# Delta-rule diagonal blocks: from DMA round trips through DRAM to VectorE transposes inside SBUF

## The chip, the cores and the metric

The kernel runs on one core of one Trainium2 chip. A core has five engines that run their own instruction streams in order and meet only at semaphores: TensorE (PE, matrix products, results in PSUM), VectorE (DVE), ScalarE (ACT), GpSimd (POOL) and SyncE (SP, which here only issues DMAs). The metric is device time in microseconds of one execution. The kernel before takes 2107.66 us (median of 3 runs, 2107.57 to 2107.68).

## The reference, cut to what matters

Two blocks of a network on 256 tokens of width 2048. The first is a hybrid layer: one large input projection, an mLSTM branch, a gated delta-rule branch, and output projections. The second is attention with context. The change touches only the delta-rule branch, 16 heads of width 128. Per head it solves a unit triangular system and then runs a recurrence:

```
kk = einsum('cbhtd,cbhsd->cbhts', kc, kc)
a_mat = where(strict, bc[..., :, None] * kk * decay_mat, 0.0)
lhs = a_mat + eye(CHUNK)
sol = triangular_solve(lhs, rhs, left_side=True, lower=True, unit_diagonal=True)
...
u = wv - einsum('bhtd,bhde->bhte', wk, S)
o = einsum('bhtd,bhde->bhte', qd, S) + einsum('bhts,bhse->bhte', qk_c, u)
S_new = ge[..., None, None] * S + einsum('bhsd,bhse->bhde', ke, u)
```

The kernel takes chunks of 128 tokens instead of 64, which gives the same result, so each head has two 128x128 triangular matrices to invert.

## The kernel before, in words

**Slots.** All weights of the projections (608 loads of 512 KB) stream through once. A part of 2048 x 512 is a *unit*, cut into 8 *slots* of 256 x 512; there are 608 slots (`SLOTS`). Per slot SP loads the tile `raw` (5 buffers), ACT copies it to a rounded `WH` (L1900), DVE writes the rest `WL` = raw - WH (L1904), and PE does 24 matmuls with 256 columns (L1960) or 12 with 512 columns (L1956). ACT and DVE prepare slot s+3 in their turn s (`AHEAD` = 3). Units 0 to 11 are `qkv`: for each group n of four heads (a *quad*) q, k and v. Units 12 to 15 are `dnz`, and more follow.

**Stages.** All other work is written as generators, one per engine; `timetable()` lists after which slots each takes its next step (a step is what stands between two `yield`s). Every engine walks the same list: slot s, then the steps planned for s. An engine that waits in a step holds everything later in its stream, its own part of the next slots too. POOL has no slot work, so for it the list only sets an order.

**The convolution stages** (`conv_*`, one per qkv unit, from the unit's last slot on): ACT copies the unit out of PSUM and scales it (L648), DVE adds three taps for each of four tiles (L683, one tile per step), ACT takes a tanh (L654), DVE writes q, k or v (L692; `vv` for v). For q and k ACT squares (L661), PE sums (L705), ACT takes the root (L666, L669) and POOL scales `qk` (L717).

**The quad stages.** Let e be the last slot of the quad's v unit. The steps lie at e+6 to e+10 and at e+20 to e+28. The next quad's q unit ends at e+8 and its k unit at e+16, so its convolution steps run between them, and e+24 is the next quad's e.

- PE: at e+7 transposes of v (L735, step `tv`), at e+8 and e+9 the score products of two heads each (L744, L745, steps `k0` to `k3`).
- POOL: at e+6 loads the decay rows `E` by DMA (L943), for quads 1 to 3 only after the last step `o1` of the quad before, since `E` is reused for `W1`, `U1` and `R2`.
- DVE: at e+7 subtracts and masks in `E` (L875, L880), ACT takes the exponential (L832); at e+8 and e+9 DVE multiplies scores and decays into `PT` and `NT` (L895, `p0` to `p3`). `NT` holds the negated triangular matrices.
- The eight 128x128 matrices have four 32x32 diagonal blocks each. SP (`quad_sp`, after `p3`) sends the 32 blocks to DRAM (L975, 8 DMAs), and reads them back so that each of the 128 partitions holds one block, four times over (L979, 4 DMAs, tile `NB`). POOL starts from unit columns `XB` (L953) and does 31 steps of forward substitution, a multiply (L960) and an add (L963) each, 62 instructions: each partition works on 8 columns of one inverse. SP sends the columns to DRAM (L985) and back into `XT` (L990), and DVE transposes them into `X` (L903, three instructions), at e+20.
- PE, ACT and DVE then join the blocks: `y5` (L756, at e+21, waits for `X`), `z5` (L768, L770), `y6` (L777), `z6` (L785), and apply the inverse and the recurrence (L792 to L820, the last at e+28). ACT (L859 to L865) and DVE (L933, step `o1`) normalise the output.

Of the kernel before, what the change touches and what calls it, by code (L numbers as in the profile page):

```python
# [96 lines left out]
def timetable():  # L97
# [13 lines left out]
    for n in range(4):  # L111
        steps(("quad", n), end("qkv", 3 * n + 2) + 6, 5)
        steps(("quad", n), end("qkv", 3 * n + 2) + 20, 9)
# [27 lines left out]


LEAD = 8
# [9 lines left out]
def hybrid_program(nc, A, out):  # L153
    with ExitStack() as ctx:
# [19 lines left out]
        def pad(n, k):  # L174
# [81 lines left out]
        Z = overlay(16 * KB,  # L256
                    [("wm0", [128, 2, 512], F32), ("wm1", [128, 2, 512], F32), ("macc", [128, 2, 512], F32)],
# [9 lines left out]
        X, XT, XB, TB, Y6, vt, U2, sq, OB = (R[n] for n in ("X", "XT", "XB", "TB", "Y6", "vt", "U2", "sq", "OB"))  # L267
# [10 lines left out]
        W1, U1, R2 = (E[:, :, 128 * i:128 * i + 128] for i in range(3))  # L278
# [278 lines left out]
        def gates_pool(e):  # L557
# [5 lines left out]
            yield  # L563

# [47 lines left out]
        def condition_dve(e):  # L612
# [111 lines left out]

        def above(B, w, h, c):

            return NT[2 * w * B:2 * w * B + w, h, 256 * c + 2 * w * B + w:256 * c + 2 * w * B + 2 * w]

        def quad_pe(e, bank, n):
            yield  # L730
# [20 lines left out]
            e.wait_ge(*qd_dve.at("x", n))  # L751
            claim(e, bank, 0, qd_act.at("y5", n))
            claim(e, bank, 1, qd_dve.at("y5", n))
            for m in range(8):
                for B in range(2):
                    p = e.matmul(SB[B][64 * B + 32:64 * B + 64, 32 * m:32 * m + 32], above(B, 32, m % 4, m // 4),  # L756
# [19 lines left out]
            for m in range(8):  # L776
                p = e.matmul(SB[0][64:128, 64 * m:64 * m + 64], above(0, 64, m % 4, m // 4), X[0:64, m, 0:64],  # L777
# [11 lines left out]
            e.wait_ge(*qd_dve.at("z6", n))  # L789
            claim(e, bank, 0, qd_dve.at("U", n))  # L790
            for h in range(4):
                m = e.matmul(SB[0][:, 128 * h:128 * h + 128], XT[:, h, :], vt[:, 0, h, :], start=True, stop=True,  # L792
                             skip_group_check=True)
# [11 lines left out]
            for h in range(4):  # L805
                m = e.matmul(SB[2][:, 128 * h:128 * h + 128], XT[:, 4 + h, :], R2[:, h, :], start=True, stop=True,
# [17 lines left out]
        def quad_act(e, n):  # L824
            yield
# [7 lines left out]
            for _ in range(5):  # L833
                yield
# [33 lines left out]
        def quad_dve(e, n):  # L868
            yield
# [15 lines left out]
            for h in range(4):  # L885
# [1325 lines left out]
```

## Time and profile before

| | |
|---|---|
| median of 3 runs | 2107.66 us |
| the profiled execution's own time | 2115.09 us |
| its span | 2113.3 us |
| PE busy | 1953.2 us (92%) |
| DVE busy | 1377.1 us (65%) |
| ACT busy | 944.5 us (45%) |
| POOL busy | 221.8 us (10%) |
| DMA mean | 187 GB/s |

The span is what the profiler sees between the first and the last instruction. The profiled execution was 7.4 us longer than the median of the unprofiled runs. PE is the engine with the most work; of its busy time most is the weight products (L1956, L1960). Its idle time and the stretches in which its clock is halved are where a change off the products can be seen.

### The profile page before, as it was taken

What the parts mean: (1) busy time and instruction counts of PE and PEld (TensorE: products, weight loads), DVE (VectorE), ACT (ScalarE), POOL (GpSimd) and SP (SyncE); (2) the same over time, 40 slices, a digit from 0 to 9 for tenths busy, and PEclk for the clock granted to TensorE, in tenths of its full rate; (3) what the DMA queues carried; (4) which work ended last, traced back from release to release, by engine and by line L of the source; (5) the groups of instructions that cost most, each with busy time, mean ns of one, the idle gap of its engine ahead of it and who ended that gap; (6) DMA issues with size and microseconds to landing.
All of it is one profiled execution on the core that took longest, in us unless ns stands there. A gap on an engine that the chain in (4) does not pass through costs nothing.

```text
span 2113.3 us, 29349 instructions
## 1 busy us (share of the span) xinstructions
PE 1953.2 (92%) x11910; PEld 1717.3 (81%) x11910; DVE 1377.1 (65%) x1919; ACT 944.5 (45%) x1336; POOL 221.8 (10%) x425
## 2 busy tenths in 40 slices
PE   5995978859699999999999999999999999999997
PEld 5995867857588889897788878898998998988875
DVE  4674555745378888787876756766455566656574
ACT  4553634434253333343444436464333345545443
POOL 1004040222201111101010100010000000011000
PEclk9997988979899999999999999999999999999998
DMA  6454443524458887767687875676556533454553
GB/s 212 131 153 117 129 132 95 172 77 151 122 193 280 270 271 256 237 221 243 227 282 253 282 262 173 218 230 198 180 169 200 179 122 128 144 166 130 170 199 120
DMA packets 198743, 395.90 MB, mean 187 GB/s; under 512 B 26136, under 2 KB 26416, under 8 KB 197456
## 3 DMA queue, kind: packets, MB, share of 16 engines
q1 hardware_dynamic: 180320, 325.63, 47.9%
q0 software_dynamic: 17424, 66.72, 10.5%
q8 instruction: 94, 1.54, 0.3%
q10 hardware_dynamic: 864, 1.67, 0.2%
q14 instruction: 41, 0.34, 0.1%
HBM read 388.70 MB, written 5.27 MB: 186 GB/s over the span
## 4 chain that ended last, share of the span: by engine, by line
PE 71%; DVE 9%; issue 8%; POOL 5%; ACT 4%; DMA 2%; SPq 1%; ACTq 0%; DVEq 0%; POOLq 0%
PE GB L1956 43%; PE GB L1960 21%; DVE WL L1904 2%; POOL XB L963 2%; POOL TB L960 2%; ACT WH L1900 2%; DVE macc L1280 1%; PE SB L357 1%; PE SB L1586 1%; PE SB L1298 1%; DVE yth L683 1%; PE SB L1578 1%; DMA wm<-in_w_mod 1%; DMA xin<-in_x 1%; DMA inverse_columns<-XB 0%
## 5 line engine op out<-in xcount | busy, mean ns | idle before, releaser
L1904 DVE TENSOR_TENSOR WL<-raw,WH 128x1024 fp32r<-128x1024 f32 x608 | 741.8, 1240 | 291.2 <-ACT WH L1900 288.7
L1900 ACT ACTIVATE WH<-raw 128x1024 fp32r<-128x1024 f32 x608 | 627.4, 1057 | 444.4 <-PE GB L1956 289.4
L1956 PE MATMUL GB<-WH,uH 128*128 128x512 f32 x896 | 283.8, 398 | 1.7 <-DVE WL L1904 1.7
L1956 PE MATMUL GB<-WH,uL 128*128 128x512 f32 x896 | 278.4, 392 | 0.0
L1956 PE MATMUL GB<-WL,uH 128*128 128x512 f32 x896 | 277.8, 391 | 0.0
L1960 PE MATMUL GB<-uH,WH 128*128 128x256 f32 x1280 | 215.7, 291 | 3.8 <-DVE WL L1904 3.8
L1280 DVE SCALAR_TENSOR_TENSOR macc<-wm,csil,macc 128x512 f32<-128x512 f32 x300 | 209.4, 747 | 5.4 <-DMA wm<-in_w_mod 3.9
L1960 PE MATMUL GB<-uL,WH 128*128 128x256 f32 x1280 | 208.7, 286 | 0.0
L1960 PE MATMUL GB<-uH,WL 128*128 128x256 f32 x1280 | 208.4, 286 | 0.0
L1956 PEld LDWEIGHTS GB<-WL,uH 128*128 128x128 f32 x896 | 169.4, 189 | 36.3
L1956 PEld LDWEIGHTS GB<-WH,uL 128*128 128x128 f32 x896 | 169.3, 189 | 36.2
L1956 PEld LDWEIGHTS GB<-WH,uH 128*128 128x128 f32 x896 | 165.7, 190 | 34.1 <-DVE WL L1904 2.6
L1960 PEld LDWEIGHTS GB<-uH,WH 128*128 128x128 f32 x1280 | 180.4, 195 | 8.5 <-issue 5.8
L1960 PEld LDWEIGHTS GB<-uL,WH 128*128 128x128 f32 x1280 | 179.7, 195 | 0.0
L1960 PEld LDWEIGHTS GB<-uH,WL 128*128 128x128 f32 x1280 | 179.5, 195 | 0.0
L1956 PE MATMUL GB<-WH,hH 128*128 128x512 f32 x512 | 162.9, 399 | 0.0
L1956 PE MATMUL GB<-WH,hL 128*128 128x512 f32 x512 | 158.2, 390 | 0.0
L1956 PE MATMUL GB<-WL,hH 128*128 128x512 f32 x512 | 157.8, 389 | 0.0
L1251 POOL DMA_DIRECT2D wm<-in_w_mod x96 | 69.5, 724 | 595.0 <-DVE macc L1280 583.4
L1956 PEld LDWEIGHTS GB<-WL,hH 128*128 128x128 f32 x512 | 96.1, 188 | 20.6
L1956 PEld LDWEIGHTS GB<-WH,hL 128*128 128x128 f32 x512 | 96.1, 188 | 20.4
L1956 PEld LDWEIGHTS GB<-WH,hH 128*128 128x128 f32 x512 | 94.4, 188 | 20.9 <-issue 3.1
(394 smaller groups left out, 2163.8 us busy)
## 6 DMA issues: line engine op xcount, KB each, us to landing
raw<-in_w_in SPq DMA_DIRECT2D x512, 512.0 KB, 4.5
wm<-in_w_mod POOLq DMA_DIRECT2D x96, 512.0 KB, 5.8
raw<-in_w_out SPq DMA_DIRECT2D x96, 512.0 KB, 5.3
xin<-in_x SPq DMA_DIRECT2D x4, 512.0 KB, 6.7
E<-decay_rows POOLq DMA_DIRECT2D x4, 512.0 KB, 5.0
NB<-diagonal_blocks SPq DMA_DIRECT2D x16, 128.0 KB, 2.6
hres<-in_x POOLq DMA_DIRECT2D x1, 2048.0 KB, 12.1
cin<-in_ctx POOLq DMA_DIRECT2D x1, 2048.0 KB, 8.6
```

The source lines that it names most:

```text
L357: t = e.transpose(SB[b][:, 256 * j + 128 * i:256 * j + 128 * i + 128], src[:, i, 128 * (2 * k + j):128 * (2 * k + j) + 128], ident[:, :])
L683: e.scalar_tensor_tensor(out=y[:, j, sh:], in0=half(banks[j // 2], j % 2)[:, 0:256 - sh], scalar=col(CONV + 48 * (3 - sh) + 16 * kind + 4 ...
L960: e.tensor_tensor(TB[:, 0:J, 0:r], NB[:, k:k + 1, k + 1:32].to_broadcast([128, J, r]), XB[:, 0:J, k:k + 1].to_broadcast([128, J, r]), mul) ...
L963: e.tensor_tensor(XB[:, 0:J, k + 1:32], XB[:, 0:J, k + 1:32], TB[:, 0:J, 0:r], add).then_inc(*qd_pool.inc(f"a{k}", n))
L1251: e.dma_start(wmr[n % 2][:, :, :], weights["w_mod"][:, 2 * i:2 * i + 2, 512 * g:512 * g + 512]).then_inc(wm_in[n % 2], 16)
L1280: w = e.scalar_tensor_tensor(out=a, in0=src, scalar=s, in1=a, op0=mul, op1=add)
L1298: m = e.matmul(SB[0][:, 4 * v + j:4 * v + j + 1], macc[:, v, 128 * j:128 * j + 128], ones[:, 0:1], start=True, stop=True, skip_group_check ...
L1578: m = e.matmul(SB[3][:, 0:128], aT[:, n % 2, 128 * q:128 * q + 128], v, start=q == 0, stop=q == 3, skip_group_check=True)
L1900: e.activation(WH[s % NH][:, :, :], raw[s % NR][:, :, :], ACT.Copy).then_inc(*wh.inc("WH", s))
L1904: e.tensor_tensor(WL[s % NH][:, :, :], raw[s % NR][:, :, :], f32(WH[s % NH][:, :, :]), sub).then_inc(*wl.inc("WL", s))
L1956: m = e.matmul(banks[j][:, :], x[:, c, 128 * j:128 * j + 128], w[:, k, :], start=first, stop=last, skip_group_check=True)
L1960: m = e.matmul(half(banks[j // 2], j % 2), w[:, k, 128 * j:128 * j + 128], x[:, c, :], start=first and j % 2 == 0, stop=last, skip_group_c ...
```

## The change

- SP no longer takes part: `quad_sp`, the two DRAM tensors and all 28 DMAs per quad go.
- ACT copies the diagonal blocks side by side into `NTd` (four instructions of 32x256), DVE spreads them with one 128x1024 transpose into `NB` (the input is read four times over). Partition 32b + 4m + g now holds block b of matrix m.
- After the substitution DVE transposes `XB` into `X` (four instructions of 32x256), and `X` into `XT` (four more). PE's `y5` waits for the first two of the eight.
- The quad's first step moves from e+7 to e+6 (the empty first step goes), and everything up to the scores with it. POOL's substitution stands at e+9, ahead of POOL's scaling of the next quad's q (L717), where it stood at e+20.
- `W1`, `U1`, `R2`, `U2` get a place of their own, so that `E` for the next quad can be loaded right behind the substitution. The modulation's first loads now wait for `o1` of quad 3 on PE, since they reuse that place.

```diff
-        steps(("quad", n), end("qkv", 3 * n + 2) + 6, 5)
+        steps(("quad", n), end("qkv", 3 * n + 2) + 6, 4)
         steps(("quad", n), end("qkv", 3 * n + 2) + 20, 9)
...
         def quad_pe(e, bank, n):
-            yield
             e.wait_ge(*cv_dve.at("dst", 3 * n + 2))
...
-            e.wait_ge(*qd_dve.at("x", n))
+            e.wait_ge(*qd_dve.at("x02", n))
...
         def quad_act(e, n):
-            yield
...
-            for _ in range(5):
-                yield
+            yield
+            yield
+            yield
+            e.wait_ge(*qd_dve.at("p3", n))
+            if n:
+                e.wait_ge(*qd_dve.at("nb", n - 1))
+            for b in range(4):
+                q = slice(32 * b, 32 * b + 32)
+                a = e.activation(NTd[q, :, :].rearrange("p (h c) r -> p h c r", c=2),
+                                 NT[q, :, :].rearrange("p h (c t) -> p h c t", c=2)[:, :, :, q], ACT.Copy)
+            a.then_inc(*qd_act.inc("nd", n))
+            yield
+            yield
...
         def quad_dve(e, n):
-            yield
...
-            yield
-            e.wait_ge(inverses_in, 64 * (n + 1))
-            for b in range(3):
+            e.wait_ge(*qd_act.at("nd", n))
+            if n:
+                e.wait_ge(*qd_pool.at("a30", n - 1))
+            e.transpose(NB[:, :, :].rearrange("p k r -> p r k"),
+                        NTd[:, :, :].rearrange("p m r -> p r m").unsqueeze(3).to_broadcast([128, 32, 8, 4]),
+                        ).then_inc(*qd_dve.inc("nb", n))
+            yield
+            e.wait_ge(*qd_pool.at("a30", n))
+            for b in (0, 2, 1, 3):
                 q = slice(32 * b, 32 * b + 32)
-                v = e.transpose(X[q, :, q], XT[q, :, q])
+                v = e.transpose(X[q, :, q].rearrange("p m (j g) -> p j m g", g=4), XB[q, :, :])
+                if b == 2:
+                    v.then_inc(*qd_dve.inc("x02", n))
             v.then_inc(*qd_dve.inc("x", n))
+            e.wait_ge(*qd_dve.at("x", n))
+            for b in (1, 3, 0, 2):
+                q = slice(32 * b, 32 * b + 32)
+                v = e.transpose(XT[q, :, q], X[q, :, q])
+                if b == 3:
+                    v.then_inc(*qd_dve.inc("xt13", n))
+            v.then_inc(*qd_dve.inc("xt", n))
...
         def quad_pool(e, n):
-            if n == 0:
-                e.wait_ge(rows_out, 32)
-                e.wait_ge(*g_dve.at("colG"))
-            else:
-                e.wait_ge(*qd_dve.at("o1", n - 1))
-            e.dma_start(E[:, :, 0:256], rowGd[4 * n:4 * n + 4, :].partition_broadcast(128)).then_inc(rowG_in, 16)
+            yield
+            yield
             yield
...
-            for _ in range(4):
-                yield
-            if n:
-                e.wait_ge(inverses_out, 64 * n)
+            else:
+                e.wait_ge(*qd_dve.at("x", n - 1))
             e.tensor_copy(XB[:, :, :], unit_cols[:, :, :]).then_inc(*qd_pool.inc("unit", n))
             e.wait_ge(*qd_pool.at("unit", n))
-            e.wait_ge(blocks_in, 64 * (n + 1))
+            e.wait_ge(*qd_dve.at("nb", n))
...
-            yield
-
-        def quad_sp(e, n):
...
+            if n < 3:
+                e.wait_ge(*qd_dve.at("p3", n))
+                decays_pool(e, n + 1)
             yield
...
                     if n == 0:
+                        e.wait_ge(*qd_pe.at("o1", 3))
                         load(0)
```

Three places show the moves. Line numbers of the changed kernel differ by a few. First DVE at the start of quad 0, before (L692 and in the changed kernel L689 write `vv`, L1904 and L1902 write `WL`):

```order
L1904 TENSOR_TENSOR WL<-raw,WH 128x1024
L692 SCALAR_TENSOR_TENSOR vv<-yth 128x1024
L1904 TENSOR_TENSOR WL<-raw,WH 128x1024 x2
L875 SCALAR_TENSOR_TENSOR E<-E,colG,mask 128x128 x4
L880 SCALAR_TENSOR_TENSOR E<-E,colG,mask 128x256 x4
L1904 TENSOR_TENSOR WL<-raw,WH 128x1024
L895 SCALAR_TENSOR_TENSOR PT<-SB,E 128x256
```

and now:

```order
L1902 TENSOR_TENSOR WL<-raw,WH 128x1024
L689 SCALAR_TENSOR_TENSOR vv<-yth 128x1024
L1902 TENSOR_TENSOR WL<-raw,WH 128x1024
L883 SCALAR_TENSOR_TENSOR E<-E,colG,mask 128x128 x4
L888 SCALAR_TENSOR_TENSOR E<-E,colG,mask 128x256 x4
L1902 TENSOR_TENSOR WL<-raw,WH 128x1024
L903 SCALAR_TENSOR_TENSOR PT<-SB,E 128x256
```

The decays stand behind one `WL` instead of two: one slot earlier in the stream. (The scores of all four heads then follow one slot earlier too, and behind the last of them, one `WL` and three taps later, stands the new `NB` transpose.)

Second, DVE at e+20 of quad 0, before:

```order
L683 SCALAR_TENSOR_TENSOR yth<-GB,vcol,yth 128x253
L903 STREAM_TRANSPOSE X<-XT 32x8x32 x3
L1904 TENSOR_TENSOR WL<-raw,WH 128x1024
L692 SCALAR_TENSOR_TENSOR qk<-yth 128x1024
L907 COPY Y<-SB 32x256
L1904 TENSOR_TENSOR WL<-raw,WH 128x1024
L910 COPY XT<-SB 32x8x32
```

and now:

```order
L680 SCALAR_TENSOR_TENSOR yth<-GB,vcol,yth 128x253
L917 STREAM_TRANSPOSE X<-XB 32x8x8x4 x4
L924 STREAM_TRANSPOSE XT<-X 32x8x32 x4
L1902 TENSOR_TENSOR WL<-raw,WH 128x1024
L689 SCALAR_TENSOR_TENSOR qk<-yth 128x1024
L930 COPY Y<-SB 32x256
L1902 TENSOR_TENSOR WL<-raw,WH 128x1024
L933 COPY XT<-SB 32x8x32
```

The step has eight transposes where it had three, and the next `WL`, the write of the next k (L689) and the copy into `Y` for `z5` stand behind all of them.

Third, POOL from the end of quad 0's substitution to the start of quad 1's, before:

```order
L960 TENSOR_TENSOR TB<-NB,XB 128x8
L963 TENSOR_TENSOR XB<-XB,TB 128x8
L717 TENSOR_TENSOR qk<-qk,sq 128x1024
L943 DMA E<-decay_rows 128x4x256
L717 TENSOR_TENSOR qk<-qk,sq 128x1024
L953 COPY XB<-unit_cols 128x256
```

and now:

```order
L980 TENSOR_TENSOR TB<-NB,XB 128x8
L983 TENSOR_TENSOR XB<-XB,TB 128x8
L961 DMA E<-decay_rows 128x4x256
L714 TENSOR_TENSOR qk<-qk,sq 128x1024 x2
L973 COPY XB<-unit_cols 128x256
L980 TENSOR_TENSOR TB<-NB,XB 128x31
```

The load of `E` has moved ahead of both scalings of `qk`, and both scalings, the next q and k of quad 1 (kinds 0 and 1), stand between two substitutions. The scaling of quad 1's q stood ahead of quad 0's substitution, that of quad 2's q ahead of quad 1's.

## Rows read from the trace of the kernel before

**Rows 1.** The page: its first line, and in part 6 the modulation's load.

```profile
span 2113.3 us, 29349 instructions
...
wm<-in_w_mod POOLq DMA_DIRECT2D x96, 512.0 KB, 5.8
```

**Rows 2.** What PE waited for: us in total, times, longest.

```profile
PE SB L756 <- DVE X L903: 92.4, 4, 24.4
...
PE SB L744 <- DVE NT L895: 7.8, 4, 3.4
```

**Rows 3.** Chain that ended last, 240 to 360 us: start, us, what.

```profile
324.76 0.43 DVE X L903
...
325.70 1.06 PE SB L756 x32
326.76 4.91 PE GB L1960 x24
...
335.37 1.72 PE SB L705 x4
...
350.02 2.87 PE GB L1960 x24
```

**Rows 4.** PE's timeline, quad 1: start, length, form, idle before it and releaser.

```profile
251.56 1.09 PE L735 MATMUL SB<-ident,vv 128*128 128x128 f32 x8 [0.36 <-DVE vv L692]
...
262.18 1.13 PE L744 MATMUL SB<-qk 128*128 128x512 f32 x2 [1.21 <-DVE NT L895]
...
264.44 0.59 PE L745 MATMUL SB<-qk 128*128 128x256 f32 x2
```

**Rows 5.** DVE's timeline, quad 1, 250 to 303 us.

```profile
250.29 1.22 DVE L692 SCALAR_TENSOR_TENSOR vv<-yth 128x1024 f32<-128x1024 f32 x1
...
255.55 1.67 DVE L880 SCALAR_TENSOR_TENSOR E<-E,colG,mask 128x256 f32<-128x256 f32 x4
...
267.49 0.74 DVE L895 SCALAR_TENSOR_TENSOR NT<-SB,colNB,E 128x256 f32<-128x256 f32 x2
...
294.54 1.22 DVE L1904 TENSOR_TENSOR WL<-raw,WH 128x1024 fp32r<-128x1024 f32 x1
295.67 1.51 DVE L683 SCALAR_TENSOR_TENSOR yth<-GB,vcol,yth 128x255 f32<-128x255 f32 x3
...
300.86 1.50 DVE L683 SCALAR_TENSOR_TENSOR yth<-GB,vcol,yth 128x255 f32<-128x255 f32 x3
```

**Rows 6.** POOL's timeline, quad 1, 287 to 325 us.

```profile
292.19 1.09 POOL L960 TENSOR_TENSOR TB<-NB,XB 128x31 f32<-128x31 f32 x1
...
294.33 0.24 POOL L960 TENSOR_TENSOR TB<-NB,XB 128x29 f32<-128x29 f32 x1
294.65 1.19 POOL L963 TENSOR_TENSOR XB<-XB,TB 128x29 f32<-128x29 f32 x1
...
317.73 0.22 POOL L963 TENSOR_TENSOR XB<-XB,TB 128x8 f32<-128x8 f32 x1
```

**Rows 7.** Lines L836 and L903: ns min/median/max, first and last start, form.

```profile
L836 ACT ACTIVATE Y<-SB x4: 375/375/378, 211.9 to 558.0; 32x256 f32<-32x256 f32 x4
...
L903 DVE STREAM_TRANSPOSE X<-XT x12: 432/434/436, 207.0 to 556.4; 32x256 f32<-32x256 f32 x12
```

**Rows 8.** PE's timeline at four other waits.

```profile
82.16 3.45 PE L705 MATMUL SB<-sq,ones 128*128 128x512 f32 x4 [2.56 <-ACT sq L661]
...
380.42 1.12 PE L744 MATMUL SB<-qk 128*128 128x512 f32 x2 [2.66 <-DVE NT L895]
...
499.44 2.08 PE L744 MATMUL SB<-qk 128*128 128x512 f32 x2 [3.43 <-DVE NT L895]
...
556.85 1.06 PE L756 MATMUL SB<-X,NT 32*32 32x32 f32 x32 [19.17 <-DVE X L903]
```

**Rows 9.** DVE's timeline, quad 3, 485 to 545 us.

```profile
505.50 0.73 DVE L895 SCALAR_TENSOR_TENSOR NT<-SB,colNB,E 128x256 f32<-128x256 f32 x2
...
527.40 5.12 DVE L1904 TENSOR_TENSOR WL<-raw,WH 128x1024 fp32r<-128x1024 f32 x4
```

More of the change, by code:

```diff
@@ L140 @@
 PLAN = timetable()
-LEAD = 8
 def take_turns(stages, s):
@@ L256, in hybrid_program @@
         Z = overlay(16 * KB,
+                    [("W1", [128, 4, 128], F32), ("U1", [128, 4, 128], F32), ("R2", [128, 4, 128], F32),
+                     ("U2", [128, 4, 128], F32), ("NTd", [128, 8, 32], F32)],
                     [("wm0", [128, 2, 512], F32), ("wm1", [128, 2, 512], F32), ("macc", [128, 2, 512], F32)],
@@ L266, in hybrid_program @@
         qk, vv, yth, E, PT, NT, NB = (R[n] for n in ("qk", "vv", "yth", "E", "PT", "NT", "NB"))
-        X, XT, XB, TB, Y6, vt, U2, sq, OB = (R[n] for n in ("X", "XT", "XB", "TB", "Y6", "vt", "U2", "sq", "OB"))
+        X, XT, XB, TB, Y6, vt, sq, OB = (R[n] for n in ("X", "XT", "XB", "TB", "Y6", "vt", "sq", "OB"))
+        W1, U1, R2, U2, NTd = (Z[n][:, :, :] for n in ("W1", "U1", "R2", "U2", "NTd"))
         s_junk, wsm, wsH, wsL, rw, xin = (R[n] for n in ("s_junk", "wsm", "wsH", "wsL", "rw", "xin"))
@@ L277, in hybrid_program @@
         fg, gmat = Z["fg"], Z["gmat"]
-        W1, U1, R2 = (E[:, :, 128 * i:128 * i + 128] for i in range(3))
         zth = yth[:, 0, :, :].rearrange("p (a b) t -> p a (b t)", a=2)
@@ L563, in gates_pool @@
             yield
+            yield
+            e.wait_ge(rows_out, 32)
+            e.wait_ge(*g_dve.at("colG"))
+            decays_pool(e, 0)
+            yield
         def newton_dve(e, says, o, v, w, root):
@@ L789, in quad_pe @@
             e.wait_ge(*qd_dve.at("z6", n))
+            e.wait_ge(*qd_act.at("z6", n))
             claim(e, bank, 0, qd_dve.at("U", n))
             for h in range(4):
-                m = e.matmul(SB[0][:, 128 * h:128 * h + 128], XT[:, h, :], vt[:, 0, h, :], start=True, stop=True,
+                m = e.matmul(SB[0][:, 128 * h:128 * h + 128], XT[:, 2 * h, :], vt[:, 0, h, :], start=True, stop=True,
                              skip_group_check=True)
@@ L805, in quad_pe @@
             for h in range(4):
-                m = e.matmul(SB[2][:, 128 * h:128 * h + 128], XT[:, 4 + h, :], R2[:, h, :], start=True, stop=True,
+                m = e.matmul(SB[2][:, 128 * h:128 * h + 128], XT[:, 2 * h + 1, :], R2[:, h, :], start=True, stop=True,
                              skip_group_check=True)
@@ L2027, in _ @@
                                 x_rows[:, i, 1024 * j:1024 * j + 1024]).then_inc(x_in[2 * i + j], 16)
-            stages = {("quad", n): quad_sp(e, n) for n in range(4)}
             for s in range(NS):
@@ L2036, in _ @@
                             weights[unit.w][:, r:r + 2, unit.col:unit.col + 512]).then_inc(raw_in[s % NR], 16)
-                if s >= LEAD:
-                    take_turns(stages, s - LEAD)
             for j in range(2):
```

46 lines of the change are left out of this document (11 added, 35 removed).

## The prediction

> **What bounds the kernel now.** I read the waits of PE first. Over the whole run one wait stands out: PE waits for `X` before `y5` four times, once per quad, 92.4 us together, 24.4 at most [rows 2]. The one of quad 3 is 19.17 us [rows 8], so the other three are 24.4 each. All other waits in the quads are small; the next is that for `p0` before `k2`, 7.8 us in four.
>
> The chain that ended last shows what lies behind it. In quad 1 it runs through POOL's substitution, SP, the DMA back into `XT`, DVE's `X` at 324.76 and PE's `y5` at 325.70 [rows 3]. The substitution takes from 292.19 to 317.95 [rows 6], and the two DMA legs behind it until the first transpose, 324.3. PE was at `y5` at 301.3 (325.70 - 24.4). DVE was there at 302.36 [rows 5] and also stood, since the wait is in its stream, so no new `WL` came either. The price is more than the idle time: the 24 products behind `y5` take 4.91 us where they take 2.87 later [rows 3], which is the half clock (1.2 instead of 2.4 GHz) for about 2 us of loss.
>
> **The change, worked out on quad 1.** I use the clock times of the profile and keep the transposes `tv` at 251.56 [rows 4] fixed. They wait for `vv`, which DVE ends at 251.5 [rows 5], and nothing ahead of `vv` changes. But `tv` now stands one slot (2.9 us) earlier in PE's stream: PE had 0.36 us to wait, now it has 3.2. This is a new wait, 4 times.
>
> 1. PE behind `tv`: 0.9, a slot 2.9, `k0`, `k1` 2.4 (in rows 4 `k2`, `k3` take from 262.18 to 264.7, where the next product starts), a slot 2.9: it is at `k2` at 260.7.
> 2. DVE: `vv` 251.5, one `WL` 1.1, decays 2.8 (in [rows 5] the last four end at 257.2 behind two `WL` and a wait for the load of `E`, which is now long done), so 255.4. ACT's exponential and `WH`, DVE's `WL` and `p0` follow: in the profile `p0` ends 4.9 behind the decays (257.2, and `k2` starts on it at 262.18), so now at 260.3, and `p1` 1.3 later. `k2` no longer waits (1.21 before, rows 4); `k3` ends at 263.1 against 264.7, one slot earlier in the stream.
> 3. `WL` 1.1, then `p2` and `p3` 2.6: 265.4, against 268.2 [rows 5].
> 4. ACT copies the blocks: 4 x 0.375 by an ACT copy of 32x256 [rows 7] = 1.5, done at 266.9. DVE does a `WL` and three taps meanwhile and is free at 268.0, so this copy is hidden; without that cover it would cost its 1.5.
> 5. The `NB` transpose. No row has one of 128x1024. Between 1.1 us (a `WL` of 1024 elements, rows 5) and 1.74 (four times 32x256 at 0.434, rows 7), and up to 3 if its strides cost. I take 1.5, near the transposes' own rate: 269.5.
> 6. The substitution. Its 62 instructions took 25.8 us [rows 6], but not evenly: the same kind of add takes 0.24 at 294.33 and 1.19 at 294.65, exactly where DVE's `WL` starts at 294.54. It happens at each `WL`, four times here, 0.9 us each, and not beside the taps (at 295.67) [rows 5]. So 25.8 - 3.6 = 22.2 us alone, of which most ran while DVE stood. Now DVE works all the time: one `WL` per slot of 2.9 us takes 0.9 away, so it becomes (22.2 + 0.9 for the write of q) / (1 - 0.9/2.9) = 33.5. End: 303.0 instead of 317.95.
> 7. DVE's own arrival at the step: 302.36 before, now 1.4 later, by the transpose and by PE's small delays ahead of the sums of squares: 303.8. So DVE, not POOL, comes last by a little. Two transposes, 0.9: `y5` at 304.7. PE is there at 263.1 + 13 slots x 2.87 + 1.7 for the sums (L705, rows 3) = 302.1. It waits 2.6 to 3.
> 8. Behind it, DVE has six more transposes (2.6), a `WL`, the write of k (1.2) and the copy for `z5` (0.4, taken as a transpose of that size, rows 7): 5.5 after `y5` starts. PE has 1.06 + 2.9 = 4.0 of work: a second new wait of 1.5. Then `z5` 0.6 and a slot, so the next L705 is at 313.7, where it was at 335.37 [rows 3]. The gain of quad 1 is 21.7 us.
>
> From there to the next `tv` nothing changes: `vv` of the next quad hangs on ACT's and DVE's normalisation behind `o1`, which starts from PE's `o1`. So the quads add up.
>
> - Quad 0: the same waits but for `k2`: 21.6.
> - Quad 2: `k2` waited 2.66 [rows 8], 1.45 more than in quad 1, and this goes too: 23.1.
> - Quad 3 lies beside `dnz` units, where DVE has few other stages, so DVE runs ahead of PE: it came to the `X` step at 532.5 [rows 9], PE at 537.7. The scores ended at 506.2 [rows 9]; they move up by most of the 3.43 us that `k2` waited and of the half clock behind it (the score matmuls took twice their time, 2.08 against 1.13 for a pair, rows 8 and 4, so 2.5 more for all), so `p3` ends near 501.2, POOL starts at 504.4, works 23 us beside DVE and 8 alone and ends at 535.7, with `X` at 536.6 and PE there at 533.5. The 19.17 become 3.1, and with the 3.43, the 2.5 and -2.9 for `tv` the gain is 19.1.
>
> Sum: 21.6 + 21.7 + 23.1 + 19.1 = 85.5 us.
>
> What works against it is PE's clock. Four long idle times become eight short ones of about 3 us. After 2.56 us of idle time PE came back at half clock (L705 took 3.45, and 1.72 in rows 3), after 2.66 it did not, after 3.43 it did [rows 8]. So at 3 us I count 6 in 10. A drop costs 1.5 to 2.5 us, say 2: for `tv` 4 x 0.6 x 2 = 4.8; for `y5` of quads 0 to 2 most of it is hidden in the wait for `z5`, 0.9 in all. This takes 5.7: gain 80.
>
> The rest costs nothing here. SP's 28 DMAs per quad go; they stood behind 10 loads of `raw`, and in the profile DVE was late only by its own wait. The load of `E` now comes behind a substitution and is needed only slots later. ACT's wait for `p3` holds a `WH` that is needed two slots later. The first loads of the modulation wait for `o1` of quad 3, three slots (8.6 us) ahead of DVE's use, and take 5.8 us [rows 1]: covered by about 2; uncovered they would cost up to 6, once.
>
> The profiled execution took 2115.09 us, 1.8 over its span of 2113.3 [rows 1] and 7.4 over the median; this would become about 2035. Taken from the median: 2107.7 - 80 = **2027 to 2028 us**; I say 2027.5.
>
> Step 5 is where a page speaks against the change. The rows show only transposes that write runs of 32 elements at 0.434 us for 256 columns [rows 7]; the new one reads and writes with a stride of 32 elements. The Trainium skill, Vector Engine (DVE) Microarchitecture Reference, section 5.2, says that a port which hops at every element costs more time per column, 1.7 to 2.5 ns instead of 1.05. By that the transpose would take an estimated 2.6 us, and the sum would fall by about 1 us per quad, 4 in all; no row here shows it.
>
> **The rivals.**
>
> *The wait only shrinks (0.17).* The substitution is slower beside a busy DVE than in step 6, since four instructions slowed by one `WL` each are all I have. If decays, writes of q and k, and the `NB` transposes cost it as well, or the 0.9 is 1.2, the 33.5 become 38 to 40, `y5` waits 8 us instead of 3 and the clock falls each time. The gain is 80 - 4 x 5 - 4 x 1 = 56: 2052. For it: step 7 has under 1 us of slack between POOL and DVE. Against it: the four excess times are alike.
>
> *All of it goes (0.12).* DVE catches up, `tv` finds the clock high, `y5` waits for nothing. Then the 92.4 us and 4 x 2.3 us of half clock come back, 101, less the `tv` waits of 4 x 2.9: about 90, 2018. Against it: `vv` really ends at 251.5.
>
> *Only the DMA legs go (0.03).* If the substitution began no earlier (317.95 to 324.3 is all that is saved), 6.4 x 4 = 26: 2082. Against it: the order has the substitution ahead of POOL's scaling, and `NB` hangs on nothing but `p3`.
>
> *Slower (0.03).* POOL comes to a near stop beside DVE: if every DVE instruction, the taps too, holds one of POOL's as long as a `WL` does, nearly each of the 62 takes 1.2 us, 76 us in all, and `y5` comes at 269.5 + 76 = 346 against 325.7: 20 us later per quad, 2187. It is slower from the point where the substitution takes 55 us. Against it: 0.24 at 294.33, with taps of DVE before and after. By the Trainium skill, GPSIMD Engine Reference, Key points, only DVE instructions with two SBUF inputs or in a two-port mode contend with POOL; the taps read one input from PSUM, and the trace agrees.
>
> **How the numbers follow.** The forecast has 0.65, the rivals 0.17, 0.12, 0.03 and 0.03. The range from 2015 to 2047 holds the forecast with its bounds (transpose up to 3 us: +6; all clock drops or none: +6, -6; POOL's 0.9 up to 1.1: +8) and the second rival, and half of the way to the first. What a measurement of this kernel can tell from no change is about 0.2%, 4 us; only the last rival is slower by more, and none lies within: faster 0.96, same 0.01, slower 0.03.
>
> **What would show it.** Right: PE's wait for `X` 2 to 5 us per quad; a wait of about 3 us before the transposes of `vv`; the substitution 31 to 36 us long, starting 3 to 5 us behind `p3`, with a slow instruction at each `WL`; a wait before `z5`. Wrong: the `NB` transpose over 3 us; PE's wait for `X` over 8; substitution under 28; new waits of PE for `WL`, which would mean that eight transposes more than fill DVE; a wait of DVE for the modulation's first load.

## The result, and the profile after

| | before | after |
|---|---|---|
| median of 4 runs each | 2107.67 us | 2039.47 us (2038.58 to 2042.45) |
| ratio, 95% interval | | 0.9679 (0.9662 to 0.9695) |
| the profiled execution, its span | 2115.09, 2113.3 us | 2042.45, 2040.6 us |
| mean granted clock | 0.969 | 0.987 |

The change takes 68.2 us off the median. The forecast was 80 us, 2027.5; the measured time lies in the range, 12 us above the forecast. Between the two profiled executions the gain is 72.64 us, since that of before lay 7.4 us over its median and that of after 3.0.

What PE waited for after (us in total, times, longest), to set beside [rows 2]:

```profile
PE SB L733 <- DVE vv L689: 12.9, 4, 3.5
PE SB L754 <- DVE X L917: 9.6, 4, 5.0
PE SB L766 <- ACT Y L845: 8.6, 3, 2.9
```

The 92.4 us for `X` are 9.6. Two waits are new or much larger: 12.9 before the transposes of v (1.9 before) and 8.6 before `z5` (none before). In what follows `tv` stands for the transposes of v, `k2` for the scores of the third head, and "the sums" for PE's sums of squares of the next quad's k (L705, now L702). PE's timeline in quad 1, where [rows 3, 4] had `tv` at 251.56, `y5` at 325.70 and the sums at 335.37:

```profile
235.15 1.97 PE L733 MATMUL SB<-ident,vv 128*128 128x128 f32 x8 [3.24 <-DVE vv L689]
...
245.95 1.02 PE L742 MATMUL SB<-qk 128*128 128x512 f32 x2
...
289.37 0.69 PE L754 MATMUL SB<-X,NT 32*32 32x32 f32 x32 [1.54 <-DVE X L917]
...
296.00 0.22 PE L766 MATMUL SB<-XT,Y 32*32 32x32 f32 x2 [2.89 <-ACT Y L845]
...
297.67 1.05 PE L1958 MATMUL GB<-uL,WH 128*128 128x256 f32 x4
...
300.12 0.64 PE L1958 MATMUL GB<-uL,WH 128*128 128x256 f32 x4
...
301.07 1.88 PE L702 MATMUL SB<-sq,ones 128*128 128x512 f32 x4
```

`k2` has no wait left, and the transposes of v take 1.97 instead of 1.09: from there to `k0` the mean granted clock is 0.68. Behind `z5` it is 0.62 up to the sums (1.05 us for four products that take 0.64 later). Between these stretches it is 1.00. PE's wait for `X` is 1.54, where 2.6 to 3 was written, since PE itself comes 2.1 us later behind `tv` than step 7 had it. DVE in the same quad, to set beside [rows 5, 7], and below it POOL, beside [rows 6]:

```profile
249.27 0.73 DVE L903 SCALAR_TENSOR_TENSOR NT<-SB,colNB,E 128x256 f32<-128x256 f32 x2
...
252.48 2.09 DVE L910 STREAM_TRANSPOSE NB<-NTd 128x1024 f32<-128x1024 f32 x1
...
288.44 1.79 DVE L917 STREAM_TRANSPOSE X<-XB 32x256 f32<-32x256 f32 x4
290.26 1.80 DVE L924 STREAM_TRANSPOSE XT<-X 32x256 f32<-32x256 f32 x4
292.10 1.23 DVE L1902 TENSOR_TENSOR WL<-raw,WH 128x1024 fp32r<-128x1024 f32 x1
293.24 1.22 DVE L689 SCALAR_TENSOR_TENSOR qk<-yth 128x1024 f32<-128x1024 f32 x1
294.49 0.43 DVE L930 COPY Y<-SB 32x256 f32<-32x256 f32 x1
```

```profile
254.72 1.00 POOL L980 TENSOR_TENSOR TB<-NB,XB 128x31 f32<-128x31 f32 x1 [43.35 <-DVE NB L910]
...
256.77 0.24 POOL L980 TENSOR_TENSOR TB<-NB,XB 128x29 f32<-128x29 f32 x1
257.08 1.19 POOL L983 TENSOR_TENSOR XB<-XB,TB 128x29 f32<-128x29 f32 x1
...
287.55 0.22 POOL L983 TENSOR_TENSOR XB<-XB,TB 128x8 f32<-128x8 f32 x1
```

The substitution runs from 254.72 to 287.77, 33.05 us, and DVE comes to `X` at 288.44 without a wait. And ACT, which decides `z5`:

```profile
294.50 1.06 ACT L658 ACTIVATE sq<-qk 128x1024 f32<-128x1024 f32 x1 [3.93 <-DVE qk L689]
295.58 0.37 ACT L845 ACTIVATE Y<-SB 32x256 f32<-32x256 f32 x1
```

Quad 3, to set beside [rows 8, 9]: the wait for `X` is 5.05 instead of 19.17, and DVE now waits for POOL.

```profile
432.64 1.58 PE L733 MATMUL SB<-ident,vv 128*128 128x128 f32 x8 [3.53 <-DVE vv L689]
...
486.44 1.07 PE L754 MATMUL SB<-X,NT 32*32 32x32 f32 x32 [5.05 <-DVE X L917]
```

```profile
444.18 1.28 DVE L1007 SCALAR_TENSOR_TENSOR yth<-yth,GB 128x512 f32<-128x512 f32 x2 [0.47 <-ACT yth L999]
...
448.29 0.74 DVE L903 SCALAR_TENSOR_TENSOR NT<-SB,colNB,E 128x256 f32<-128x256 f32 x2
...
485.50 1.80 DVE L917 STREAM_TRANSPOSE X<-XB 32x256 f32<-32x256 f32 x4 [9.24 <-POOL XB L983]
```

**Three stretches.** A quad's time on PE can be cut at three marks: `tv` to `y5`, `y5` to the sums, and from there to the next `tv`. In quad 1, in us, by the starts in PE's timeline, with the experiments that follow. The experiments ran in three groups (e1 to e4, e5 to e8, e9 to e12), each beside the kernel before, whose median was 2107.66, 2106.85 and 2107.13; so differences of a us or so between groups are not a result.

| kernel | tv to y5 | y5 to sums | to next tv | median, us |
|---|---|---|---|---|
| before | 74.14 | 9.51 | 33.1 | 2107.67 |
| after (e1_same) | 54.15 | 11.72 | 33.1 | 2038.95 |
| e2, copies first | 54.18 | 8.78 | 33.1 | 2030.80 |
| e3, and ahead of `WL` | 54.22 | 8.80 | 33.1 | 2031.34 |
| e4, tv with scores | 52.76 | 11.74 | 33.1 | 2037.41 |
| e5, start a step late | 53.73 | 11.73 | 33.1 | 2038.03 |
| e6, half the substitution | 53.91 | 11.70 | 33.1 | 2031.73 |
| e7, flat `NB` transpose | 53.75 | 11.60 | 33.3 | 2037.37 |
| e8, DMA but early | 64.54 | 8.72 | 33.5 | 2082.47 |
| e9, in SBUF but late | 69.81 | 10.24 | 33.1 | 2083.87 |
| e10, e2 and e4 | 52.78 | 8.79 | 33.1 | 2028.10 |
| e11, e2 and e5 | 53.75 | 8.80 | 33.1 | 2032.16 |
| e12, e10 and X first | 52.19 | 14.05 | 33.1 | 2041.00 |

The third stretch stays within 0.4 us. The forecast for the first two was 53.14 and 9.0.

### The profile page after: what moved, and what is told of

It reads as the page before. It is cut to its first block, busy times and chain, and to the rows that moved or that the text cites. A ratio compares the mean times of both kernels' runs of the same rounds, so it can differ in the third digit from the quotient of the medians.

```text
span 2040.6 us, 29310 instructions
## 1 busy us (share of the span) xinstructions
PE 1953.3 (96%) x11910; PEld 1719.4 (84%) x11910; DVE 1389.8 (68%) x1943; ACT 952.0 (47%) x1352; POOL 248.0 (12%) x425
## 3 DMA queue, kind: packets, MB, share of 16 engines
q0 software_dynamic: 17424, 66.72, 10.8%
q8 instruction: 94, 1.54, 0.3%
## 4 chain that ended last, share of the span: by engine, by line
PE 77%; DVE 11%; ACT 5%; issue 4%; POOL 1%; DMA 1%; SPq 0%; ACTq 0%; DVEq 0%; POOLq 0%
PE GB L1954 44%; PE GB L1958 24%; DVE WL L1902 3%; ACT WH L1898 2%; DVE yth L680 2%; DVE macc L1278 1%; PE SB L352 1%; PE SB L1584 1%; PE SB L1296 1%; POOL TB L980 1%; PE SB L1576 1%; POOL XB L983 1%; DMA wm<-in_w_mod 1%; PE SB L742 1%; DMA xin<-in_x 1%
## 5 line engine op out<-in xcount | busy, mean ns | idle before, releaser
L1902 DVE TENSOR_TENSOR WL<-raw,WH 128x1024 fp32r<-128x1024 f32 x608 | 738.5, 1234 | 286.3 <-ACT WH L1898 283.6
```

The costliest lines, as they stand in the source:

```text
L1902: e.tensor_tensor(WL[s % NH][:, :, :], raw[s % NR][:, :, :], f32(WH[s % NH][:, :, :]), sub).then_inc(*wl.inc("WL", s))
```

## The experiments

My theory after the comparison: the shortfall is (a) the chain to `y5`, about 1 us longer, and (b) `z5`, which waits for a copy that ACT makes late, with half clock behind it. The rivals: POOL and DVE slow each other so that POOL bounds all quads; or the loss is in the new early place of `tv`.

**e1, the changed kernel again.**

> The changed kernel again, with nothing edited: the base of this group. Its median was 2039.5 us, 0.9679 of the kernel before with an interval of 0.9662 to 0.9695. With more rounds it should be 2038 to 2041 us, and its waits the same: PE before the transposes of v 12.9 us in four, before y5 9.6 in four, before z5 8.6 in three.

2038.95 us (2038.62 to 2039.22), ratio 0.9677 (0.9663 to 0.9690). The waits are 12.9 before `tv` and 10.7 before `y5`, but that before `z5` fell from 8.6 to 4.2 without any gain:

```profile
287.09 0.69 PE L754 MATMUL SB<-X,NT 32*32 32x32 f32 x32 [1.53 <-DVE X L917]
287.72 0.74 PE L1958 MATMUL GB<-uH,WH 128*128 128x256 f32 x4
...
289.74 1.05 PE L1958 MATMUL GB<-uH,WH 128*128 128x256 f32 x4
...
293.73 0.22 PE L766 MATMUL SB<-XT,Y 32*32 32x32 f32 x2 [1.38 <-ACT Y L845]
```

This time the clock fell behind `y5` as well, after the same wait of 1.53 us, and the slower products filled part of the wait. `z5` stands 6.64 us behind `y5` in both, and in both half clock follows it (a mean of 0.63 here).

**e2, the copies of y5 first.** In the step e+21 the quad's part stands ahead of the convolution's:

```diff
+    for n in range(4):
+        plan[end("qkv", 3 * n + 2) + 21].sort(key=lambda stage: stage != ("quad", n))
```

> ACT copies y5 ahead of the square of the k unit, in the same step; nothing moves on the other engines. Theory (z5 waits for ACT's copy, which stands behind a square that waits for DVE's write of k): ACT's copy now ends near 290.9 instead of 295.95, z5 then waits for DVE's copy, which ends at 294.9, so the wait falls from 2.89 to about 1.8, the 1.5 of the prediction and a little. 1.05 us in each of three quads, and the half clock behind z5 (1.6 us each) goes where the shorter wait doesn't bring it: 3 to 8 us in all, 2031 to 2036 us. Rival (PE would wait for DVE anyway, or the clock and the substitution decide): under 2 us.

2030.80 us (2030.60 to 2032.54), ratio 0.9640 (0.9626 to 0.9653): 8.2 us less than e1, just beyond the upper end of the theory (8 us, 2031). The expectation was wrong on the order: DVE's copy moved too, ahead of the write of k. So both copies came in time and the wait went wholly:

```profile
285.33 1.80 DVE L926 STREAM_TRANSPOSE XT<-X 32x256 f32<-32x256 f32 x4
287.16 1.22 DVE L1904 TENSOR_TENSOR WL<-raw,WH 128x1024 fp32r<-128x1024 f32 x1
288.42 0.43 DVE L932 COPY Y<-SB 32x256 f32<-32x256 f32 x1
```

```profile
284.43 0.69 PE L756 MATMUL SB<-X,NT 32*32 32x32 f32 x32 [1.53 <-DVE X L919]
285.06 0.96 PE L1960 MATMUL GB<-uH,WH 128*128 128x256 f32 x4
...
289.61 0.22 PE L768 MATMUL SB<-XT,Y 32*32 32x32 f32 x2
```

The gain is 2.9 in quad 1. The half clock did not go, it moved: `y5` to `z5` takes 5.18 us with it, and `z5` to the sums 3.60 without it, where after had 5.07.

**e3, DVE's copy ahead of `WL` as well.**

```diff
             v.then_inc(*qd_dve.inc("xt", n))
-            yield
             e.wait_ge(*qd_pe.at("y5", n))
             e.tensor_copy(Y5[96:128, :, :], ...).then_inc(*qd_dve.inc("y5", n))
             yield
+            yield
```

> As the run before, and DVE copies its half of y5 directly behind the transposes of X, ahead of the WL and of the write of k. Theory: DVE's copy ends near 292.5, ACT's at 290.9, PE is at z5 at 293.1, so no wait and no half clock: 2.9 + 1.6 us in each of three quads and up to 2 in quad 3, 12 to 15 us in all, about 2026 us. Rival (DVE is full, and 0.4 us taken ahead of a WL come back as a wait for WL, or as a later write of k and a wait for the sums of squares): the gain is under 6 us and a new wait of PE of over 0.5 us for WL or sq appears in each quad.

2031.34 us (2029.58 to 2032.70): no difference from e2, which had left almost nothing to wait for. The theory's 12 to 15 us were too many, since they counted half clock. Quad 2 shows what that half clock is worth now: there none fell behind `y5` (granted clock 1.00, `z5` 3.69 us behind `y5`), and the sums still came 8.53 behind `y5`, against 8.80 in quad 1 with half clock. PE waited for ACT's copy of `X` out of the bank instead:

```profile
388.76 1.96 PE L704 MATMUL SB<-sq,ones 128*128 128x512 f32 x4 [1.08 <-ACT X L852]
```

So with the copies in time ACT's and DVE's chain sets this stretch, to about 0.3 us. The rival's wait (over 0.5 us in each quad) came in one quad only.

**e4, tv beside the first scores.** PE's first `yield` is back, and the one between `tv` and `k0` is gone.

> PE transposes v one slot later, where the kernel before has it, and then computes the first two scores at once; every other engine keeps the changed order. Theory (the early place costs a wait of 3.24 and 0.9 of half clock): the wait falls to about 0.4 and the transposes take 1.1 instead of 2.0, but k2 stands one slot behind and comes at 241.5, where p0 ends at 243.8 on DVE, so 2.3 us come back as a wait for p0; k3 ends near 246.3 instead of 248.3. 2 us in each of four quads if the clock stays up, none if it falls: 2031 to 2039 us. Rival (the time between the transposes of v and p3 is DVE's and ACT's chain, PE's place does not matter): same within 2 us. Third (the wait of 3.24 simply goes, k2 isn't held): 4 us in each quad, 2023.

2037.41 us (2036.38 to 2038.61): 1.5 us less than e1, whose fastest run was 2038.62. Of the 12.9 us before `tv` 0.4 are left in quad 1, but there are 4.9 before `k2`, 3.3 for ACT's copies of v, and 12.1 instead of 10.7 for `X`:

```profile
PE SB L754 <- DVE X L917: 12.1, 4, 6.2
...
PE SB L742 <- DVE NT L903: 4.9, 4, 1.3
...
PE SB L742 <- ACT vt L828: 3.3, 4, 0.8
```

`tv` to `y5` shrinks by 1.4. The third theory (the wait simply goes, 2023) is refuted; the second, that DVE's and ACT's chain decides, holds within its 2 us, and the first held in part. But `y5` is not indifferent to the place: from `tv` of quad 0 to `tv` of quad 3 the trace takes 292.05 us, 296.45 in e1. Of these 4.4 us the medians show 1.5; the rest is lost outside these marks, and the traces do not say to what.

**e5, the quad's start a step late.**

```diff
-        steps(("quad", n), end("qkv", 3 * n + 2) + 6, 4)
+        steps(("quad", n), end("qkv", 3 * n + 2) + 7, 4)
```

> The changed kernel with the first four steps of a quad back at e+7, where the kernel before has them; the substitution still begins one step behind the scores, and all later steps stay. Theory (the way from vv to y5 is a chain of DVE, ACT and POOL, and PE only waits in it at one place or another): the wait before the transposes of v falls from 3.24 to about 0.4 and k2 waits 1.2, p3 ends at tv + 16.6 instead of 14.8, POOL at tv + 54.4, y5 at tv + 56.0 instead of 54.2, and PE's wait there grows from 1.5 to about 7 us. 1.8 us later in each quad: 2046 us (2042 to 2050). Rival (the wait before the transposes of v is a loss that could be had back): about 2026 to 2032. Second rival (the early start is a large part of the gain): 11 us (a step of 2.9 in each quad) or more lost, 2051.

2038.03 us (2035.31 to 2043.08): no difference. All three theories missed; mine expected 7 us of loss. The trace shows why:

```profile
252.45 1.00 POOL L980 TENSOR_TENSOR TB<-NB,XB 128x31 f32<-128x31 f32 x1 [44.46 <-DVE NB L910]
...
284.30 0.22 POOL L983 TENSOR_TENSOR XB<-XB,TB 128x8 f32<-128x8 f32 x1
```

```profile
284.55 1.80 DVE L917 STREAM_TRANSPOSE X<-XB 32x256 f32<-32x256 f32 x4 [0.82 <-POOL XB L983]
```

With `tv` at 231.76 POOL starts 20.7 us behind it, not 19.5 (in e1 252.45 - 232.94), works 32.1 us instead of 33.0 (11 of its instructions are slow, 12 in e1), and DVE, in e1 0.7 us late by itself, now waits 0.82 for POOL. So 1.2 us of later start cost nothing in quads 0 to 2. In quad 3, where POOL comes last, `y5` stands 55.91 us behind `tv` instead of 53.32; that it costs nothing in the median is within the spread of these four runs, 8 us. The step to e+6 is worth little here; what helps is where the substitution stands (e9).

**e6, 16 of 31 steps of the substitution.**

```diff
-            for k in range(31):
+            for k in range(16):
```

> POOL makes the first 16 of the 31 steps of the substitution; the others, and with them part of the result, are left out. POOL is then done about 16 us before DVE comes to the X step. Theory (in quads 0 to 2 DVE comes last, by 0.75 us, in quad 3 POOL): y5 of quads 0 to 2 still waits 0.9 to 1.5 us, since DVE's two transposes stand before it; in quad 3 the wait of 5.05 to 6.18 goes and its half clock; and the WLs of quads 0 to 2 don't move. 4 to 8 us in all against the repeated changed kernel, 2031 to 2035. Rival (POOL is what bounds all four quads, through its end or through slowing DVE): the waits go in all quads, with those before z5, 4 us or more in each, 2022 or below.

2031.73 us (2030.20 to 2033.24), 7.2 us less than e1:

```profile
286.06 0.69 PE L754 MATMUL SB<-X,NT 32*32 32x32 f32 x32 [1.47 <-DVE X L917]
...
477.85 0.69 PE L754 MATMUL SB<-X,NT 32*32 32x32 f32 x32
```

In quads 0 to 2 the wait stays, 1.47 us, with POOL done 15 us earlier behind `tv`; in quad 3 it goes, and `tv` to `y5` there is 48.7 instead of 53.3 us. So DVE, not POOL, comes last ahead of `y5` in three quads and POOL in one, as the theory has it; the rival is refuted.

**e7, the block transpose in runs.**

```diff
-            e.transpose(NB[:, :, :].rearrange("p k r -> p r k"),
-                        NTd[:, :, :].rearrange("p m r -> p r m").unsqueeze(3).to_broadcast([128, 32, 8, 4]),
+            e.transpose(NB[:, :, :].rearrange("p (a b) r -> p a (b r)", a=4),
+                        NTd[:, :, :].rearrange("p m r -> p (m r)").unsqueeze(1).to_broadcast([128, 4, 256]),
```

> DVE's transpose into NB reads and writes runs of 32 elements and more instead of single elements with a stride of 32; what stands in NB is then ordered wrongly, and so are the values behind it, the work is the same. If the stride sets its 2.09 us, it takes 1.7 (4 x 0.434, the rate of the 32x256 transposes) or as little as 1.1, and POOL starts 0.4 to 1.0 earlier. In quads 0 to 2 this moves DVE as well, so y5 comes 0.4 to 1.0 earlier: 1.5 to 4 us in all, 2035 to 2037.5. Rival (the width sets it: 1024 columns at 2.0 ns however they are ordered): 2.09 again and the same time as the repeated changed kernel, 2039.

2037.37 us (2037.11 to 2038.05): 1.6 us less than e1, but in another group; the ratios, 0.9669 (0.9652 to 0.9685) and 0.9677 (0.9663 to 0.9690), do not tell them apart. The trace does. The line's ns (min/median/max), first in this kernel, then in the changed one:

```profile
L910 DVE STREAM_TRANSPOSE NB<-NTd x4: 1235/1236/1245, 151.3 to 445.9; 128x1024 f32<-128x1024 f32 x4
```

```profile
L910 DVE STREAM_TRANSPOSE NB<-NTd x4: 2072/2092/2134, 153.4 to 450.8; 128x1024 f32<-128x1024 f32 x4
```

The stride costs 0.86 us, of which 0.4 reaches `y5` in quad 1. The rival (the width sets it) is refuted by the duration.

**e8, the kernel before with an early substitution.** DMAs kept:

```diff
-            for _ in range(4):
+            for _ in range(2):
                 yield
```

> The kernel before, its DMAs kept, with POOL's substitution two steps earlier in the order, ahead of the scaling L717 that waits for ACT until 288. Theory (the late start of POOL is the larger part of the 92 us of waits, the DMA legs the smaller): the blocks are in NB near 280, POOL starts there instead of at 292.2, makes 15 of its 22 us beside DVE until 302 and the rest alone, done near 309 instead of 318; y5 comes 8 to 9 us earlier in each quad: 2070 to 2077 us. Rival (only the legs matter, and beside a busy DVE the early start gives nothing): under 10 us, 2098 or above. Second rival (the legs overlap with other waits, and nearly all lies in the start): 2050 or below.

2082.47 us (2077.32 to 2084.90), 24.4 us less than before's 2106.85 in that group, and above the 2070 to 2077 of the theory; both rivals are refuted.

```profile
305.58 1.06 PE L756 MATMUL SB<-X,NT 32*32 32x32 f32 x32 [15.51 <-DVE X L903]
```

The waits for `X` are 15.5 in quads 0 to 2, 8.9 less each, as expected; in quad 3, where no scaling stood ahead, 19.1 as before. I had counted four quads.

**e9, inside SBUF but late.** One more `yield` ahead of POOL's substitution in the changed kernel.

> The changed kernel with POOL's substitution one step later in the order, which puts it behind the scaling that waits for ACT's exponential, as in the kernel before; blocks and inverses still travel without DMA. The scaling ends at tv + 41.7 (as in the run with half the steps), the substitution starts there instead of at tv + 19.5, runs 11.7 us beside a working DVE (8 us of its 22.8 alone) and the rest alone, and ends at tv + 68; y5 comes at tv + 69.6 instead of 54.1, in quads 0 to 2. Quad 3 has no scaling and stays. Theory (neither half gives much alone: 22 and 24 us, together 69): 3 x 15.4 = 46 us are lost, 2085 us. Rival (the DMAs were most of it): 2060 or below. Second rival (without the early start nothing is left of the gain): 2095 or above.

2083.87 us (2082.37 to 2086.05), where 2085 was expected; `y5` stands 69.8 us behind `tv`:

```profile
287.00 2.41 POOL L714 TENSOR_TENSOR qk<-qk,sq 128x1024 f32<-128x1024 f32 x1 [64.44 <-ACT sq L666]
...
290.82 1.09 POOL L981 TENSOR_TENSOR TB<-NB,XB 128x31 f32<-128x31 f32 x1
```

**Together, e8 and e9 split the change.** By the medians transport alone gives 23 us (e9, which keeps the rest of the change too), the early place alone 24, both 68. But the two do not work in the same quads. What each quad gained against before, from `tv` to the next `tv` and in quad 3 from `tv` to `y6`, in us, from one trace each:

| kernel | quad 0 | quad 1 | quad 2 | quad 3 |
|---|---|---|---|---|
| e8, early place alone | 9.2 | 10.1 | 11.2 | 3.2 |
| e9, transport alone | 3.1 | 3.6 | 4.6 | 16.5 |
| both, the change | 17.6 | 17.7 | 20.0 | 16.9 |

In quad 3 no scaling stands ahead of the substitution, and transport alone gives nearly all. In quads 0 to 2 each half hides behind the other, for 4 to 5 us each by these rows: with the scaling ahead, the blocks' way in by DMA is covered by POOL's wait for ACT; with DMA, POOL stands early but its blocks come 8.5 us later (269.15 - 241.04 = 28.1 behind `tv`, against 19.6). The medians put the surplus of both over the sum of the two at about 20 us. The traced executions put it lower, since that of before lay 7.4 us above its median and that of e8 5.1 below.

**e10, e2 and e4 together: the version that beats both kernels.**

> The two edits that helped, together: ACT's and DVE's copies of y5 ahead of the square and of the write of k, and the transposes of v with the first scores. If they add: 2038.95 - 8.15 - 1.5 = 2029.3 us. Theory (PE's waits before the transposes, before k2, before y5 and before z5 share one chain that begins with vv; what is taken from PE's part ahead of y5 comes back as a wait for X, but behind y5 there is nothing left to wait for): 2028 to 2030. Rival (without the wait before z5 the time ahead of y5 comes through in full, 4 us per quad): 2018 or below.

2028.10 us (2025.36 to 2029.30), ratio 0.9625 (0.9611 to 0.9639) to before, 10.9 us less than e1. All runs of e2 lie above all of these, but in another group, and the intervals of the two ratios overlap (e2: 0.9626 to 0.9653). The time is what adding gives (2029.3), as expected; the rival (2018) is refuted. The edits are those of e2 and e4.

**e11, e2 and e5 together.**

> The copies of y5 ahead, and the first four steps of a quad back at e+7. The late start alone cost nothing (2038.0 against 2038.95), since POOL worked 1 us shorter and DVE stood 0.8 less late than thought. Theory: the same again, 2030 within 2 us, with PE's wait for X at 3.2 in quads 0 to 2. Rival (the late start was hidden only behind the wait before z5): 1.5 to 2 us more in each quad, 2036.

2032.16 us (2029.72 to 2033.38), just over the 2 us allowed, but with runs that overlap those of e2. `X` waited 3.2 us in quads 0 to 2, as expected.

**e12, e10 with X ahead of the taps.** The same sort for e+20 too.

> As the run with both edits, and DVE transposes X ahead of three taps of the same step (1.5 us). Nothing moves on the other engines. In the changed kernel DVE came to X 0.7 us behind POOL's end, so X can come 0.7 us earlier and then waits for POOL. Theory (then POOL comes last, DVE has no more to give): 0.7 in each of three quads, 2 us in all, 2027. Rival (the taps that are now 3.6 us later hold the tanh, the write of k and the sums of squares): a new wait of PE for sq of 1 us or more in each quad, and no gain, 2029 or above.

2041.00 us (2040.50 to 2041.91), 12.9 us worse than e10. `y5` comes 0.6 us earlier, as the theory has it, and 5.3 us are lost behind it. The rival named the right cause, the later taps, but not the wait: it is `z5`'s (4.34 us, with no releaser given), which starts as DVE's copy ends, and PE has no new wait for the sums:

```profile
289.75 1.52 DVE L683 SCALAR_TENSOR_TENSOR yth<-GB,vcol,yth 128x255 f32<-128x255 f32 x3
293.33 1.22 DVE L1905 TENSOR_TENSOR WL<-raw,WH 128x1024 fp32r<-128x1024 f32 x1 [2.07 <-ACT WH L1901]
294.59 0.43 DVE L933 COPY Y<-SB 32x256 f32<-32x256 f32 x1
```

```profile
295.12 0.26 PE L769 MATMUL SB<-XT,Y 32*32 32x32 f32 x2 [4.34 <-issue]
```

ACT's tanh needs the taps and holds `WH`; DVE's `WL` waits for that, and the copy for `z5` stands behind it.

## Why the prediction was right or wrong

**Right in mechanism.** In quads 0 to 2 the wait for `X` falls to one that DVE and not POOL ends, by under 1 us (step 7; e6 shows it), and in quad 3 to one that POOL ends. The substitution took 33.05 us where step 6 had 33.5: 12 of its 62 instructions took 1.0 to 1.3 us, at the 11 `WL` beside it and at the write of q, so 22.2 us of work alone and 0.9 us for each of the 12. `k2`'s wait went (step 2), ACT's copy of the blocks was hidden (step 4: 1.70 us), and the wait before `tv` was 3.24 where 3.2 was written. Step 7's wait of 2.6 to 3 for `X` was 1.54: PE came 2.1 us late, 1.7 of it by `k2`, through half clock behind `tv`.

**The sum.** From `tv` to the sums quads 0 to 2 gained 17.6, 17.7 and 19.7 us, where 21.6, 21.7 and 23.1 were forecast; quad 3, to `y6`, 16.9 where 19.1 was. That is 71.9 against 85.5 less 5.7 for the clock. In quad 1 `tv` to the sums took 65.92 us where 62.14 was written: the 3.8 missing are 1.1 ahead of `y5` and 2.7 behind it.

- *Step 8 failed, and is the larger part.* It had PE's wait before `z5` at 1.5, by DVE's copy, which came 5.55 us behind `y5`, as written (5.5). But the wait was 2.89, and `z5` stood 6.63 behind `y5`: ACT has a copy of its own, behind a square that waits for DVE's write of k, and that stands behind the eight transposes. The step never asked what stood ahead of the other half of the copy. Before the change ACT's copy began 3.4 us behind `y5`, with three transposes ahead of it, and PE came 6.0 behind `y5`, after 24 products of which most were at half clock [rows 3]; with eight transposes ahead the copy begins 6.2 behind. The other part of the 2.7 is half clock behind `z5`, for which the step had no term: from `z5` to the sums 5.07 us passed, where 3.5 was written. In quad 0 of e5 and of e6 `z5` stands 6.63 behind `y5` as well, but at full clock behind it, and `y5` to the sums takes 10.24; so the late copy costs 1.2 and the half clock 1.5. e2 takes the wait away and the stretch is 8.8, near the 9.0 of the forecast, though made of half clock and not of a wait.
- *Step 5 was mis-sized.* 2.09 us, where 1.5 was taken and 1.74 was the bound of the rows. e7 puts the stride's share at 0.86, of which only 0.4 reached `y5`. The 1.74 was no rate either: 0.434 us for 256 columns and 1.236 for 1024, both in runs, make an estimate of 1.04 ns per column and 0.17 us for each instruction. The Trainium skill, Vector Engine (DVE) Microarchitecture Reference, section 5.2, gives 1.7 to 2.5 ns per column for a port that hops at every element. The trace has 2.04, and 1.21 with runs, so the trace agrees and the page spoke rightly against the change; the estimate of 2.6 us taken from it was its upper end.
- *Step 1's place of `tv`* costs more than its wait. Through the half clock `k2` and `k3` come late enough (10.8 us behind `tv`, where 9.1 was written) that DVE waits 1.24 us for them before `p2`. e4, with `tv` a slot later at full clock, has `y5` 1.4 us earlier.
- *Quad 3.* `p3` ended at 449.0, 16.4 us behind `tv`, where 14.4 was forecast: the `dnz` stage's instructions (L1007, L1012) stand between `p1` and `p2`. POOL starts 20.4 behind `tv` instead of 17.6, and the wait is 5.05 instead of 3.1.
- *The clock* fell at `tv` in all four quads of the first profile, where 6 in 10 was counted: `k0` stands 5.30 to 5.38 us behind `tv`, and 3.69 where it did not fall (e1, quad 3), so 1.6 us each and not 2. Behind `z5` it fell in three quads at 1.5 each, where 0.9 in all was deducted. The deduction of 5.7 covers a part of the 13.6 missing. It is right in kind, and that the measured time lies no further off is in part its luck: it was placed at `tv` and `y5`, and 4.5 us of what the half clock cost lay behind `z5`.
- The last 4.4 us between 72.64 and 68.2 are the profiled executions' own distance from their medians, which the forecast took as equal.

*Wrong in the text on record:* it says that 28 DMAs per quad go. They are 20 (8, 4, 4 and 4). No number rested on it. The first loads of the modulation cost nothing, as written: they start at 517.65, 14.9 us ahead of their use.

**The rivals.** "The wait only shrinks" had a loss of 24 us against the forecast, by a slower POOL; it was 12, and POOL was not slower. "Only the DMA legs go" did not come either. It priced the transport alone at 26 us and e9 has 23, but not by its mechanism: 6.4 us in each quad were written, and e9's trace has 3 to 5 in quads 0 to 2 and 16.5 in quad 3. "All of it goes" and "slower" did not come.

What stays open: why the clock falls behind one wait of 1.53 us and not behind another of the same length (e1 and after, quad 1), nor behind one of 3.53 us before `tv` (e1, quad 3), where it fell in after. The cost of the early `tv` was shown with its position and its clock together, not apart.

## What to carry to other kernels

When a step gets longer on one engine, look at every engine that must deliver to the next step, and at what stands ahead of its delivery: here two copies of 0.4 us behind another stage's work cost 8 us, and two lines that change the order within a step gave them back. Two halves of a change can be worth 23 and 24 us alone and 68 together, when each stall covers the other; so price a chain with both removed, not by adding, and look at each stage by itself: where only one of the two stalls exists (quad 3), the other half gives little. A wait that is only moved upstream, or an earlier start of a chain that ends on another engine, is worth nothing until the chain's last engine gets it.

## What the runs showed of the hardware

- A DVE transpose of 128x1024 took 2.09 us with single elements at a stride of 32 and 1.24 us with runs; one of 32x256 in runs took 0.43.
- One POOL instruction took about 0.9 us more beside each DVE instruction of 128x1024 with two SBUF inputs (`WL`, and once the write of `qk` at 265.38: 1.16), and none did beside taps that read PSUM. The same 62 instructions took 25.8 us with 4 slow ones (before), 28.8 with 7 (e8), 32.1 with 11 (e5) and 33.05 with 12.
- After a wait of 3.24 us PE's transposes took 1.97 us in one execution and 1.09 in another; in the second the time from `tv` to `k0` was the same, 5.30 against 5.35, since the half clock came a little later. Without half clock it was 3.7 to 3.8. One instruction's length is no measure of what a clock drop costs; the distance between two marks is.
